# Streaming the expert weights past stationary tokens in the gate and up products of a mixture-of-experts layer

## The chip, the core and the metric

The kernel runs on one core of a Trainium2 chip. The metric is the device time of one launch in microseconds, the median of several runs. The engines of the core are named as in the profile: PE (TensorE, matrix products), PEld (its weight loads), DVE (VectorE), ACT (ScalarE), POOL (GpSimd) and SP (SyncE, which here only issues transfers). "Slot" means a 512 KB piece of on-chip memory that holds 128 rows of one expert's weights.

## The reference, cut to what matters

One layer of a diffusion backbone on 640 tokens of 1024 numbers, all float32. The part that the change touches is the grouped top-2 mixture of 16 experts at the end of the layer:

```python
def expert_block(args):
    xe, e = args
    return (jax.nn.silu(xe @ w_gate[e]) * (xe @ w_up[e])) @ w_down[e]
```

Every token goes to two experts. The rows are sorted by expert, padded to whole blocks, and each block is run through its expert's three 1024x1024 matrices. The rest of the layer (two token mixers, norms, router) comes before, and the weighted sum of each token's two rows and the last norm come after.

## The kernel before, in words

All engines run their own instruction list and meet at semaphores. The first 1100 us hold the mixers, the output projection and the router. Then the expert stage begins.

**Blocks.** The kernel cuts an expert's tokens into blocks of `MB` = 64. With this input there are 28 blocks; experts 0 to 15 have 1, 1, 1, 1, 2, 2, 2, 2, 4, 1, 3, 4, 1, 1, 1, 1 of them. Nine experts have one block, seven have two or more (19 blocks). The blocks run in the order of the experts.

**PE, lines 1566 to 1612.** For each block a loop over f (eight groups of 128 hidden columns) makes the gate and the up product for that f: the weights are the stationary operand, 128 rows by 64 columns at a time, and the 64 tokens stream (`mm` at L1603, 32 products for an f: 2 matrices, 8 row groups k, 2 halves of the array's columns). The result has hidden columns on partitions, so ACT applies silu (L711), DVE multiplies (L1222), and the product is at once the stationary operand of the down product `down(f)` (L1588), which runs one f behind: two products, each 64 tokens stationary and 512 weight columns streaming, one in either half of the array. At f = 7 the next block's tokens are transposed (`transpose_x`, L1571), and ACT copies them out (L702). Each float32 product is two records in the trace.

**Weights, lines 407 to 427.** An expert has 24 slots of 512 KB: for each f one of gate, one of up, one of down. There is one set of slots. SP issues the loads of the next expert in the order gate f, up f, down f: it waits until the last block of the expert before has used gate and up of f (`gu_done`), issues those two, waits for `down_done` of f, issues the third. SP issues strictly in its written order. PE waits at `gu_in[f]` and `dn_in[f]`. The first expert's loads wait for `h2_ready`, the last three of them for `x_scattered`.

**POOL, lines 470 to 545.** Early in the kernel it fills the sorted input rows and part of the output rows with zeros by transfers of 64 rows, and waits for them before it builds `m_lhs` (L487 to L494), which the scan of the first mixer (DVE, L905 to L913) doesn't need but runs beside. In the expert stage it loads the tokens of each block and stores the results `y_block`.

Of the kernel before, what the change touches and what calls it, by code (L numbers as in the profile page):

```python
# [26 lines left out]
ALU = mybir.AluOpType  # L27
ACT = mybir.ActivationFunctionType
AX = mybir.AxisListType

P = 128
# [57 lines left out]
def hybrid_step(nc, x_t, x_rows, pos_rows, small, const, masks, stream, w_out, norm_f, hg_state, router_w,  # L89
                w_gate, w_up, w_down, y_rows, s5_new, hg_new):  # L90
    ctx = ExitStack()
    with ctx:
# [116 lines left out]
        w_slot = [at(f"expert_w{s}", end - (s + 1) * 4096, [P, KD, P]) for s in range(3 * KF)]  # L209
        x_blk = at("x_block", qs0, [P, D])  # L210
        x_blk_t = at("x_block_t", qs0 + 4096, [P, KD, MB])
        act_t = at("act_t", qs0 + 8192, [P, KF, MB])
        y_blk = at("y_block", qs0 + 12288, [P, 512])
        silu = at("silu_tmp", qs0 + 16384, [P, 2, MB])
# [96 lines left out]
        silu_ready = sem("silu_ready")  # L311
        x3_ready = sem("x3_ready")
# [59 lines left out]
        def _(sp):  # L372
# [34 lines left out]
            sp.wait_ge(h2_ready, CH)  # L407
            for f in range(KF):
                if f == KF - 1:
                    sp.wait_ge(x_scattered, 16 * 2 * CH)  # L410
                sp.dma_start(w_slot[3 * f][:, :, :], w_gate[0, f, :, :, :]).then_inc(gu_in[f], 16)
                sp.dma_start(w_slot[3 * f + 1][:, :, :], w_up[0, f, :, :, :]).then_inc(gu_in[f], 16)
                sp.dma_start(w_slot[3 * f + 2][:, :, :], w_down[0, f, :, :, :]).then_inc(dn_in[f], 16)
            sp.wait_ge(route_ready, 1)
            with sp.Fori(1, EXPERTS) as e:
                b = sp.value_load(rint[0:1, bass.ds(e + START, 1)], min_val=0, max_val=NBLK)
                for f in range(KF):

                    sp.wait_ge(gu_done, b * KF + (f + 1))
                    sp.dma_start(w_slot[3 * f][:, :, :], w_gate[bass.ds(e, 1), f, :, :, :]  # L420
                                 .rearrange("a p k c -> p (a k) c")).then_inc(gu_in[f], 16)
                    sp.dma_start(w_slot[3 * f + 1][:, :, :], w_up[bass.ds(e, 1), f, :, :, :]
                                 .rearrange("a p k c -> p (a k) c")).then_inc(gu_in[f], 16)

                    sp.wait_ge(down_done, b * KF + (f + 1))
                    sp.dma_start(w_slot[3 * f + 2][:, :, :], w_down[bass.ds(e, 1), f, :, :, :]
                                 .rearrange("a p k c -> p (a k) c")).then_inc(dn_in[f], 16)
# [20 lines left out]
        def _(pool):  # L448
# [22 lines left out]
            for b in range(NBLK + 1):  # L471
# [1278 lines left out]
```

## Time and profile before

| | us |
|---|---|
| runs | 1858.84, 1854.5, 1855.0; median 1855.0 |
| profiled execution | 1854.49 |
| its span (first to last instruction) | 1852.9 |
| first gate product to end of the last down product | 1106.08 to 1804.77 |
| PE busy over the span | 1547.5 (84%) |
| gate and up products, busy / mean of one record | 460.7 / 0.224 |
| down products, busy / mean of one record | 229.7 / 0.602 |

The span is 1.6 us shorter than the execution's own time, which is 0.5 us below the median. Busy times of PE overlap: a product is counted from its start to the end of its result, so cadence is read from the starts in the timeline and not from the mean. The profile's chain of waits puts 63% of the span on PE, 19% on DVE and 9% on DMA.

### The profile page before, as it was taken

Reading aid. Unit: us, or ns where it says so; the run is one execution under the profiler, and the core shown is the slowest. Engines: PE = TensorE matmul, PEld = TensorE weight load, DVE = VectorE, ACT = ScalarE, POOL = GpSimd, SP = SyncE. Lnnn points to the kernel's source line nnn. Section 1 sums busy time; section 2 is a strip of 40 time slices with the busy share of each in tenths; the row PEclk is TensorE's granted clock in tenths of the full one; section 3 lists DMA queues with packets and bytes.
Section 4 is the critical chain, followed back from the end, with each engine's and each line's share of the span. In section 5 each row is a group of like instructions: output and inputs, shape, how many; then the busy total and the mean of one; then the engine's idle time right before and its main releaser. Section 6 shows DMA issues by size and latency. Waiting matters only on the chain.

```text
span 1852.9 us, 46239 instructions
## 1 busy us (share of the span) xinstructions
PE 1547.5 (84%) x20214; PEld 1206.8 (65%) x20215; DVE 581.4 (31%) x1109; ACT 265.2 (14%) x463; POOL 187.6 (10%) x212
## 2 busy tenths in 40 slices
PE   7598994997576787999989819889999998999770
PEld 7376793997466675777744617657777776777550
DVE  3812994002678855111153221001111110111006
ACT  2014000001322222000001101111111111111012
POOL 0043581001000000000000020000000000000002
PEclk9798996666789998999999759999999999999995
DMA  9059505123201110122301469988887194719984
GB/s 349 26 146 235 137 24 103 57 69 86 74 24 57 46 62 30 46 69 68 159 12 57 174 226 395 397 338 297 301 300 285 51 396 158 296 27 393 396 349 175
DMA packets 90295, 319.19 MB, mean 172 GB/s; under 512 B 11489, under 2 KB 14817, under 8 KB 89985
## 3 DMA queue, kind: packets, MB, share of 16 engines
q1 hardware_dynamic: 72288, 270.05, 38.8%
q0 software_dynamic: 14496, 46.77, 9.3%
q10 hardware_dynamic: 3456, 1.57, 0.8%
q8 instruction: 42, 0.69, 0.1%
q14 instruction: 13, 0.10, 0.0%
HBM read 283.46 MB, written 32.80 MB: 171 GB/s over the span
## 4 chain that ended last, share of the span: by engine, by line
PE 63%; DVE 19%; DMA 9%; SPq 4%; issue 3%; ACT 1%; ACTq 1%; POOL 1%; POOLq 0%; DVEq 0%
PE ps L1603 18%; PE ps L1277 13%; PE ps L1588 8%; DMA expert_w<-in_w_up 7%; PE ps L1295 4%; PE ps L1520 4%; PE ps L1540 4%; PE ps L1481 3%; DVE block_states L913 2%; DVE scan_tmp L905 2%; DVE scan_tmp L911 2%; PE ps L1418 2%; SPq L420 1%; DVE node_x L1044 1%; DVE node_x L1043 1%
## 5 line engine op out<-in xcount | busy, mean ns | idle before, releaser
L1603 PEld LDWEIGHTS ps<-x_block_t,expert_w 128*64 128x64 f32 x14336 | 453.5, 139 | 176.0 <-issue 105.0
L1603 PE MATMUL ps<-x_block_t,expert_w 128*64 128x64 f32 x14336 | 460.7, 224 | 49.2 <-DMA expert_w<-in_w_up 46.0
L1277 PE MATMUL ps<-h_t,weight_ring 128*128 128x320 f32 x1152 | 319.3, 438 | 21.0 <-DVE h_t L884 21.0
L1277 PEld LDWEIGHTS ps<-h_t,weight_ring 128*128 128x128 f32 x1152 | 222.2, 193 | 115.8 <-DVE h_t L884 21.5
L1222 DVE TENSOR_TENSOR act_t<-silu_tmp,ps 128x64 f32<-128x64 f32 x224 | 49.6, 222 | 596.6 <-ACT silu_tmp L711 596.6
L1588 PE MATMUL ps<-expert_w,act_t 128*64 128x512 f32 x896 | 229.7, 602 | 0.0
L711 ACT ACTIVATE silu_tmp<-ps 128x64 f32<-128x64 f32 x224 | 50.0, 223 | 583.0 <-PE ps L1603 583.0
L1295 PE MATMUL ps<-c_silu,weight_ring 128*128 128x128 f32 x768 | 123.8, 333 | 11.3 <-DMA weight_ring<-in_stream 11.3
L1295 PEld LDWEIGHTS ps<-c_silu,weight_ring 128*128 128x128 f32 x768 | 117.8, 244 | 12.1 <-issue 6.8
L1481 PE MATMUL ps<-node_x 128*128 128x128 f32 x560 | 73.3, 288 | 42.2 <-DVE node_x L1044 24.3
L1481 PEld LDWEIGHTS ps<-node_x 128*128 128x128 f32 x560 | 67.7, 199 | 47.8 <-DVE node_x L1044 27.0
L540 POOL DMA_DIRECT2D y_sorted<-y_block x56 | 29.9, 534 | 512.6 <-DVE y_block L1226 509.9
L1540 PE MATMUL ps<-w_out_sb,merged 128*128 128x512 f32 x160 | 68.8, 592 | 0.0
L524 POOL DMA_INDIRECT x_sorted<-h,router_ints x10 | 9.6, 962 | 558.5 <-DVEq L1215 555.8
L1588 PEld LDWEIGHTS ps<-expert_w,act_t 128*64 128x64 f32 x896 | 48.2, 139 | 17.9 <-issue 16.0
L1540 PEld LDWEIGHTS ps<-w_out_sb,merged 128*128 128x128 f32 x160 | 30.4, 190 | 38.3 <-issue 38.1
L648 ACT ACTIVATE exp_tmp<-exp_tmp 128x2560 f32<-128x2560 f32 x16 | 37.4, 2337 | 121.5 <-DVE exp_tmp L1035 59.9
L1571 PE MATMUL ps<-constants,x_block 64*128 64x64 f32 x232 | 20.9, 232 | 32.8 <-DMA x_block<-x_sorted 32.8
L941 DVE TENSOR_SCALAR k_fwd<-f_fwd 128x2560 f32<-128x2560 f32 x1 | 1.5, 1495 | 141.4 <-PE ps L1422 141.4
L913 DVE TENSOR_TENSOR block_states<-scan_tmp,scan_tmp 128x64 f32<-128x64 f32 (+1 forms) x63 | 42.3, 672 | 2.1
L1015 DVE COPY_PREDICATED att<-masks,ps 128x256 f32<-128x256 uint8 x70 | 35.1, 523 | 25.1 <-PE ps L1481 25.0
L1571 PEld LDWEIGHTS ps<-constants,x_block 64*128 64x128 f32 x232 | 16.9, 141 | 34.9 <-DMA x_block<-x_sorted 33.0
(301 smaller groups left out, 1451.9 us busy)
## 6 DMA issues: line engine op xcount, KB each, us to landing
expert_w<-in_w_gate SPq DMA_DIRECT2D x128, 512.0 KB, 13.5
expert_w<-in_w_up SPq DMA_DIRECT2D x128, 512.0 KB, 14.7
expert_w<-in_w_down SPq DMA_DIRECT2D x128, 512.0 KB, 14.2
weight_ring<-in_stream SPq DMA_DIRECT2D x98, 512.0 KB, 3.6
x_sorted<-zero POOLq DMA_DIRECT2D x36, 256.0 KB, 20.5
x_block<-x_sorted POOLq DMA_DIRECT2D x29, 256.0 KB, 6.6
y_sorted<-y_block POOLq DMA_DIRECT2D x56, 128.0 KB, 5.1
y_sorted<-zero POOLq DMA_DIRECT2D x19, 256.0 KB, 40.0
```

Of the source, the lines that this page charges most:

```text
L648: nc.scalar.activation(ex[:, :, :], ex[:, :, :], ACT.Exp).then_inc(e_exp, 1)
L711: nc.scalar.activation(silu[:, f % 2, :], ps[:, f % 2, 0:MB], ACT.Silu).then_inc(silu_ready, 1)
L913: done(vec.tensor_tensor(h_out, t1, t2, ALU.add))
L1222: vec.tensor_tensor(act_t[:, f, :], silu[:, f % 2, :], ps[:, 2 + f % 2, 0:MB], ALU.mult)\
L1277: last = mm(pair(job)[:, a, :], w[:, k, :], h_t[:, k, a * HALF:(a + 1) * HALF], start=(k == 0), stop=(k == KD - 1))
L1295: last = mm(bank(job)[:, 2 * j:2 * j + P], w[:, k, :], bc(csil[:, k, :], 1, P // 2), start=(k == 0), stop=(k == KD - 1))
L1481: last = mm(bank(job)[:, h * P:(h + 1) * P], both, both, start=True, stop=True)
L1520: last = mm(bank(job)[:, 0:HALF], br[:, 4 * w + k, :], y[:, k, a * HALF:(a + 1) * HALF], start=(k == 0), stop=(k == 3))
L1540: last = mm(bank(job), merged[:, k, c * P:(c + 1) * P], wo[:, k, 512 * half:512 * half + 512], start=(k == 0), stop=(k == KD - 1))
L1571: last = nc.tensor.transpose(ps[:, 6, k * MB:(k + 1) * MB], x_blk[0:MB, k * P:(k + 1) * P], ident[0:MB, 0:MB])
L1588: last = mm(ps[MB * half:MB * half + MB, 4, :], act_t[:, f, :], w_slot[3 * f + 2][:, 4 * half:4 * half + 4, :].rearrange("p k c -> p (k c) ...
L1603: last = mm(ps[cols, 2 * w + f % 2, 0:MB], w_slot[3 * f + w][:, k, cols], x_blk_t[:, k, :], start=(k == 0), stop=(k == KD - 1))
```

## The change

The expert stage is written in another way, and three things around it move.

- **Gate and up.** The tokens `x_block_t` are now the stationary operand, 64 columns, and 512 weight columns stream. For each of eight row groups k there are four products: two halves of the columns, and gate in the upper half of the array's columns, up in the lower. The result has tokens on partitions (gate in 0 to 63, up in 64 to 127), over two banks. ACT copies it to `gate_up_rows`, PE turns it with eight 128x128 transposes (`turn_rows`), ACT applies silu to all 512 columns at once, DVE multiplies all 512 at once.
- **Down.** The down product of block i-1 runs in iteration i, behind the gate and up products and the token transposes of block i. The first block's gate and up stand ahead of the loop, the last block's down behind it.
- **Weights.** A gate or up slot now holds 128 input rows of all 1024 columns. SP issues all 16 gate and up loads of an expert, each pair behind `gu_done` of the last block before, and then its 8 down loads, each behind `down_done`.
- **Around it.** The first expert's first 12 loads wait for `x2_ready` and no longer for `h2_ready`; the slots and the small tiles have other addresses. The zero fill goes by 128 rows (28 transfers, before 55). POOL stores the result of a block in the next iteration.

```diff
-            sp.wait_ge(h2_ready, CH)
+            sp.wait_ge(x2_ready, CH)
+            for k in range(KD):
+                if 2 * k == 12:
+                    sp.wait_ge(h2_ready, CH)
+                sp.dma_start(w_slot[2 * k][:, :], w_gate[0, k, :, :]).then_inc(gu_in[k], 16)
+                sp.dma_start(w_slot[2 * k + 1][:, :], w_up[0, k, :, :]).then_inc(gu_in[k], 16)
             for f in range(KF):
                 if f == KF - 1:
                     sp.wait_ge(x_scattered, 16 * 2 * CH)
-                sp.dma_start(w_slot[3 * f][:, :, :], w_gate[0, f, :, :, :]).then_inc(gu_in[f], 16)
-                sp.dma_start(w_slot[3 * f + 1][:, :, :], w_up[0, f, :, :, :]).then_inc(gu_in[f], 16)
-                sp.dma_start(w_slot[3 * f + 2][:, :, :], w_down[0, f, :, :, :]).then_inc(dn_in[f], 16)
+                sp.dma_start(w_slot[2 * KD + f][:, :], w_down[0, f, :, :]).then_inc(dn_in[f], 16)
...
             with sp.Fori(1, EXPERTS) as e:
-                b = sp.value_load(rint[0:1, bass.ds(e + START, 1)], min_val=0, max_val=NBLK)
+                last = sp.value_load(rint[0:1, bass.ds(e + START, 1)], min_val=0, max_val=NBLK)
+                for k in range(KD):
+
+                    sp.wait_ge(gu_done, last * KD + (k + 1))
+                    sp.dma_start(w_slot[2 * k][:, :], w_gate[bass.ds(e, 1), k, :, :]
+                                 .rearrange("a p c -> p (a c)")).then_inc(gu_in[k], 16)
+                    sp.dma_start(w_slot[2 * k + 1][:, :], w_up[bass.ds(e, 1), k, :, :]
+                                 .rearrange("a p c -> p (a c)")).then_inc(gu_in[k], 16)
                 for f in range(KF):
-                    sp.wait_ge(gu_done, b * KF + (f + 1))
...
-                    sp.wait_ge(down_done, b * KF + (f + 1))
...
+                    sp.wait_ge(down_done, last * KF + (f + 1))
+                    sp.dma_start(w_slot[2 * KD + f][:, :], w_down[bass.ds(e, 1), f, :, :]
+                                 .rearrange("a p c -> p (a c)")).then_inc(dn_in[f], 16)
...
-            for b in range(NBLK + 1):
-                pool.dma_start(x_sorted[b * MB:(b + 1) * MB, :], zero[0:MB, :]).then_inc(zeroed, 16)
+            for r in range(0, X_ROWS, P):
+                pool.dma_start(x_sorted[r:r + P, :], zero[:, :]).then_inc(zeroed, 16)
...
+            def rows():
+                nc.scalar.activation(gu_rows[:, :, :], ps[:, 0:2, :], ACT.Copy).then_inc(gu_taken, 1)
+
+            def gate():
+                nc.scalar.activation(silu[:, :, :].rearrange("p (a c) t -> p a c t", a=2),
+                                     ps[:, 2:4, :].rearrange("p a (c n) -> p a c n", c=4)[:, :, :, 0:MB], ACT.Silu)\
+                    .then_inc(silu_ready, 1)
...
+            with act.Fori(1, NBLK) as i:
                 with act.If(i < blocks):
...
+                    act.wait_ge(gu_done, i * KD + KD)
+                    rows()
                     act.wait_ge(xt_done, i + 2)
                     copy_x()
+                    act.wait_ge(prod_ready, i)
+                    act.wait_ge(gu_turned, i + 1)
+                    gate()
...
+            def turn_rows():
+                for f in range(KF):
+                    last = nc.tensor.transpose(ps[:, 2 + f // 4, f % 4 * P:f % 4 * P + P],
+                                               gu_rows[:, f // 4, f % 4 * P:f % 4 * P + P], ident)
+                last.then_inc(gu_turned, 1)
+
+            def gate_up(come, x_come):
+                for k in range(KD):
+                    pe.wait_ge(gu_in[k], come)
+                    if k == KD - 1:
+                        pe.wait_ge(x_blk_in, x_come)
+                    for h in range(2):
+                        for w in range(2):
+                            last = mm(ps[MB * w:MB * w + MB, h, :], x_blk_t[:, k, :],
+                                      w_slot[2 * k + w][:, 512 * h:512 * h + 512], start=(k == 0), stop=(k == KD - 1))
+                    last.then_inc(gu_done, 1)
+
+            def down(come):
+                for f in range(KF):
+                    pe.wait_ge(dn_in[f], come)
+                    for h in range(2):
+                        last = mm(ps[MB * h:MB * h + MB, 4, :], act_t[:, f, :],
+                                  w_slot[2 * KD + f][:, 512 * h:512 * h + 512], start=(f == 0), stop=(f == KF - 1))
+                    last.then_inc(down_done, 1)
...
+            pe.wait_ge(xt_copied, 1)
+            gate_up(32, 32)
+            transpose_x()
+            pe.wait_ge(gu_taken, 1)
+            turn_rows()
+            with pe.Fori(1, NBLK) as i:
                 with pe.If(i < blocks):
...
+                    gate_up(e * 32 + 32, i * 16 + 32)
+                    transpose_x()
+                    before = pe.value_load(rint[0:1, bass.ds(i - 1, 1)], min_val=0, max_val=EXPERTS - 1)
+                    pe.wait_ge(prod_ready, i)
+                    pe.wait_ge(y_copied, i)
+                    down(before * 16 + 16)
+                    pe.wait_ge(gu_taken, i + 1)
+                    turn_rows()
                 pe.nop()
+            pe.wait_ge(prod_ready, blocks)
+            pe.wait_ge(y_copied, blocks)
+            down(16 * EXPERTS)
```

**SP, the loads of the next expert.** In the loop over experts, SP's instructions before; `in_w_gate`, `in_w_up` and `in_w_down` are the three matrices in memory, and each row is one slot's load. The other six f read the same.

```order
L420 ISA [waits gu_done]
L420 DMA expert_w_126<-in_w_gate 128x1024
L422 DMA expert_w_127<-in_w_up 128x1024
L426 DMA expert_w_128<-in_w_down 128x1024 [waits down_done]
L419 REGISTER_ALU
L420 ISA [waits gu_done]
L420 DMA expert_w_129<-in_w_gate 128x1024
L422 DMA expert_w_130<-in_w_up 128x1024
L426 DMA expert_w_131<-in_w_down 128x1024 [waits down_done]
```

The same loop now, from the last gate and up pair to the loop's end and back.

```order
L428 ISA [waits gu_done]
L428 DMA expert_w_140<-in_w_gate 128x1024
L430 DMA expert_w_141<-in_w_up 128x1024
L435 DMA expert_w_142<-in_w_down 128x1024 [waits down_done]
L435 DMA expert_w_143<-in_w_down 128x1024 [waits down_done]
L435 DMA expert_w_144<-in_w_down 128x1024 [waits down_done]
L435 DMA expert_w_145<-in_w_down 128x1024 [waits down_done]
L435 DMA expert_w_146<-in_w_down 128x1024 [waits down_done]
L435 DMA expert_w_147<-in_w_down 128x1024 [waits down_done]
L435 DMA expert_w_148<-in_w_down 128x1024 [waits down_done]
L435 DMA expert_w_149<-in_w_down 128x1024 [waits down_done]
L423 REGISTER_ALU
```

What moved: the down loads stood among the gate and up loads, and now stand behind all of them; the next expert's first gate load stands behind the eighth down load.

**PE, a block's iteration.** Before, at the first two f of a block (L1603 gate and up, L1588 down).

```order
L1603 MATMUL ps<-x_block_t,expert_w_126 64x64 x16
L1603 MATMUL ps<-x_block_t,expert_w_127 64x64 x16
L1603 MATMUL ps<-x_block_t,expert_w_129 64x64 x16
L1603 MATMUL ps<-x_block_t,expert_w_130 64x64 x16
L1583 ISA
L1584 ISA
L1588 MATMUL ps<-expert_w_128,act_t 64x512 x2
L1603 MATMUL ps<-x_block_t,expert_w_132 64x64 x16
L1603 MATMUL ps<-x_block_t,expert_w_133 64x64 x16
```

Now, from the eighth row group of gate and up (L1635) to the second step of down (L1643, slots 142 and 143).

```order
L1632 ISA [waits gu_in7]
L1635 MATMUL ps<-expert_w_140,x_block_t 64x512 [waits x_blk_in]
L1635 MATMUL ps<-expert_w_141,x_block_t 64x512
L1635 MATMUL ps<-expert_w_140,x_block_t 64x512
L1635 MATMUL ps<-expert_w_141,x_block_t 64x512
L1618 MATMUL ps<-constants,x_block 128x64 x8
L1661 TENSOR_LOAD router_ints
L1641 ISA [waits y_copied,prod_ready]
L1643 MATMUL ps<-expert_w_142,act_t 64x512 [waits dn_in0]
L1643 MATMUL ps<-expert_w_142,act_t 64x512
L1643 MATMUL ps<-expert_w_143,act_t 64x512 [waits dn_in1]
```

What moved: 16 products of 64 columns for each slot became two of 512 columns, and the first down product of a block stands behind the whole gate and up of the next block.

## Rows read from the trace of the kernel before

**Rows 1.** The page's part 5: busy us, mean ns of one; idle before, releaser

```profile
L1603 PE MATMUL ps<-x_block_t,expert_w 128*64 128x64 f32 x14336 | 460.7, 224 | 49.2 <-DMA expert_w<-in_w_up 46.0
...
L1588 PE MATMUL ps<-expert_w,act_t 128*64 128x512 f32 x896 | 229.7, 602 | 0.0
```

**Rows 2.** Timeline of PE, a block without waits: start us, us, engine, line, op

```profile
1253.16 2.04 PE L1603 MATMUL ps<-x_block_t,expert_w 128*64 128x64 f32 x64
1255.02 1.03 PE L1588 MATMUL ps<-expert_w,act_t 128*64 128x512 f32 x4
1255.88 2.04 PE L1603 MATMUL ps<-x_block_t,expert_w 128*64 128x64 f32 x64
...
1268.75 0.71 PE L1571 MATMUL ps<-constants,x_block 64*128 64x64 f32 x8
1269.39 1.94 PE L1588 MATMUL ps<-expert_w,act_t 128*64 128x512 f32 x8
1271.15 1.04 PE L1603 MATMUL ps<-x_block_t,expert_w 128*64 128x64 f32 x30
```

**Rows 3.** Busy us by stretches (PE, PEld, DVE, ACT, POOL), then clock, DMA share, GB/s

```profile
1247.00:1269.50 22.50, 22.50 (x554) 17.76 (x552) 2.46 (x9) 3.58 (x11) 1.60 (x3) 1.00 0.82 288
1728.00:1760.00 32.00, 24.29 (x526) 17.95 (x523) 2.46 (x9) 3.67 (x10) 1.59 (x3) 0.95 1.03 400
```

**Rows 4.** Timeline of SP, the first loads of experts 14 and 15

```profile
1720.15 3.03 SPq L420 DMA_DIRECT2D expert_w<-in_w_gate  x1
...
1753.57 2.64 SPq L420 DMA_DIRECT2D expert_w<-in_w_gate  x1
```

**Rows 5.** Waits of SP's queue: us in total, times, longest

```profile
SPq L420 <- PE ps L1603: 276.0, 8, 67.6
SPq L426 <- PE ps L1588: 92.1, 71, 3.3
```

**Rows 6.** The slots' loads, from issue to landing

```profile
DMA to landing us min/median/max: 3.5/14.2/18.6
```

**Rows 7.** Timeline of PE, the start of the expert stage

```profile
1106.08 6.02 PE L1603 MATMUL ps<-x_block_t,expert_w 128*64 128x64 f32 x128 [0.77 <-ACT x_block_t L702]
```

**Rows 8.** 128x128 transposes at the full clock: ns min/median/max, first and last start

```profile
L1334 PE MATMUL ps<-constants,g_pre x64: 272/273/273, 146.1 to 153.0; 128*128 128x128 f32 x64
```

**Rows 9.** The chain of waits, eight 128x128 transposes at the half clock

```profile
1044.24 1.98 PE ps L1548 x8
```

**Rows 10.** ACT's copy of 128x1024 out of PSUM

```profile
L580 ACT ACTIVATE g_lhs<-ps x8: 1026/1054/1102, 147.2 to 153.5; 128x1024 f32<-128x1024 f32 x8
```

**Rows 11.** Timeline, the last block's down product and the copy of its result

```profile
1802.83 1.94 PE L1588 MATMUL ps<-expert_w,act_t 128*64 128x512 f32 x8
1802.93 0.60 ACT L702 ACTIVATE x_block_t<-ps 128x512 f32<-128x512 f32 x1 [0.41 <-PE ps L1571]
...
1804.90 0.69 DVE L1226 COPY y_block<-ps 128x512 f32<-128x512 f32 x1 [2.12 <-PE ps L1588]
```

**Rows 12.** Timeline of PE, two steps behind a wait for weights

```profile
1726.99 2.08 PE L1603 MATMUL ps<-x_block_t,expert_w 128*64 128x64 f32 x64 [2.36 <-DMA expert_w<-in_w_up]
...
1755.92 3.56 PE L1603 MATMUL ps<-x_block_t,expert_w 128*64 128x64 f32 x64 [2.33 <-DMA expert_w<-in_w_up]
```

**Rows 13.** Timeline of POOL, the zero fill and what waits for it

```profile
126.04 18.69 POOL L472 DMA_DIRECT2D x_sorted<-zero  x36 [0.29 <-POOL zero L470]
...
204.32 4.36 POOL L487 TENSOR_TENSOR m_lhs<-small_params,powers 128x2304 f32<-128x2304 f32 x1 [48.86 <-DMA y_sorted<-zero]
```

**Rows 14.** Timeline of DVE, the scan as POOL starts

```profile
204.30 0.22 DVE L911 TENSOR_TENSOR scan_tmp<-scan_tmp,block_states 128x64 f32<-128x64 f32 x1
204.55 4.21 DVE L913 TENSOR_TENSOR block_states<-scan_tmp,scan_tmp 128x64 f32<-128x64 f32 x1
```

**Rows 15.** Timeline of PE during the zero fill

```profile
162.47 5.93 PE L1347 MATMUL ps<-u_blocks,g_lhs 128*64 128x80 f32 x128 [3.43 <-issue]
172.52 1.06 PE L1347 MATMUL ps<-u_blocks,g_lhs 128*64 128x80 f32 x10 [4.11 <-issue]
```

More of the change, by code:

```diff
@@ L311, in hybrid_step @@
         silu_ready = sem("silu_ready")
+        gu_taken = sem("gu_taken")
+        gu_turned = sem("gu_turned")
         x3_ready = sem("x3_ready")
@@ L531, in _, with store_y @@
             blocks = pool.value_load(rint[0:1, TOTAL:TOTAL + 1], min_val=EXPERTS, max_val=NBLK)
-            with pool.Fori(0, NBLK) as i:
+            def store_y(row):
+                for half in range(2):
+                    pool.dma_start(y_sorted[bass.ds(row, MB), 512 * half:512 * half + 512],
+                                   y_blk[MB * half:MB * half + MB, :]).then_inc(y_stored, 16)
+            pool.wait_ge(xt_done, 1)
+            pool.dma_start(x_blk[0:MB, :], x_sorted[MB:2 * MB, :]).then_inc(x_blk_in, 16)
+            with pool.Fori(1, NBLK) as i:
                 with pool.If(i < blocks):
@@ L703, in copy_x @@
                     .then_inc(xt_copied, 1)
+            def rows():
[4 more added lines that the diff above has]
+                    .then_inc(silu_ready, 1)
             act.wait_ge(xt_done, 1)
             copy_x()
-            with act.Fori(0, NBLK) as i:
+            act.wait_ge(gu_done, KD)
+            rows()
+            act.wait_ge(xt_done, 2)
+            copy_x()
+            act.wait_ge(gu_turned, 1)
+            gate()
+            with act.Fori(1, NBLK) as i:
                 with act.If(i < blocks):
-                    for f in range(KF):
-                        act.wait_ge(gu_done, i * KF + f + 1)
-                        nc.scalar.activation(silu[:, f % 2, :], ps[:, f % 2, 0:MB], ACT.Silu).then_inc(silu_ready, 1)
+                    act.wait_ge(gu_done, i * KD + KD)
+                    rows()
                     act.wait_ge(xt_done, i + 2)
                     copy_x()
+                    act.wait_ge(prod_ready, i)
+                    act.wait_ge(gu_turned, i + 1)
+                    gate()
                 act.nop()
@@ L1217, in _, with product, take_y @@
             blocks = dve.value_load(rint[0:1, TOTAL:TOTAL + 1], min_val=EXPERTS, max_val=NBLK)
[L1218 to L1226 removed]
+            def product():
+                vec.tensor_tensor(act_t[:, :, :].rearrange("p (a c) t -> p a c t", a=2),
+                                  silu[:, :, :].rearrange("p (a c) t -> p a c t", a=2),
+                                  ps[:, 2:4, :].rearrange("p a (c n) -> p a c n", c=4)[:, :, :, MB:2 * MB], ALU.mult)\
+                    .then_inc(prod_ready, 1)
+            def take_y():
+                vec.tensor_copy(y_blk[:, :], ps[:, 4, :]).then_inc(y_copied, 1)
+            dve.wait_ge(silu_ready, 1)
+            product()
+            with dve.Fori(1, NBLK) as i:
+                with dve.If(i < blocks):
+                    dve.wait_ge(down_done, i * KF)
+                    dve.wait_ge(y_free, i)
+                    take_y()
+                    dve.wait_ge(silu_ready, i + 1)
+                    product()
                 dve.nop()
+            dve.wait_ge(down_done, blocks * KF)
+            dve.wait_ge(y_free, blocks)
+            take_y()
             w_of = rt[:, N_GS, 20:30]
```

83 lines of the change are left out of this document (22 added, 61 removed).

## The prediction

> **What bounds the kernel now.** I read four views, in this order. The page's part 5 first: the two largest groups of the stage are the gate and up products and the down products, and PE's idle time before the first is put down to the loads of up weights [rows 1]. Then the timeline of PE over one block that waits for nothing. The reader is to see the cadence in the starts: an f of gate and up takes 1.86 us (1253.16 to 1255.02), one of down 0.86 (1255.02 to 1255.88), the eight token transposes 0.64, and two steps of down 1.76 [rows 2]. A block is 8 x 1.86 + 8 x 0.86 + 0.64 + 0.2 for the loop = 22.6 us. 28 such blocks are 632.5 of the stage's 698.7 us (1106.08 to 1804.77). The other 66 are waits for weights, and the third view shows where. In the stretches, a block in the middle of many-block experts has PE busy throughout; in the stretch of single-block experts DMA is full at 400 GB/s and PE is busy 24.3 us of 32 [rows 3]. SP starts the loads of expert 14 at 1720.15 and of expert 15 at 1753.57 [rows 4]: 33.4 us for 24 loads, 1.39 us each. That is the floor of a single-block expert while the queue never runs empty. Fourth, SP's waits: eight long ones for gate and up, ahead of each expert whose loads wait through several blocks, and 71 short ones for down, 3.3 us at most [rows 5]. So the stage has two bounds: PE's 22.6 us a block where an expert has several, DMA's 33.4 us where it has one.
>
> **The change, part by part.** The sum runs from the first gate product to the end of the last down product.
>
> *Gate and up.* A k step is four products in the shape of today's down: 64 columns stationary, 512 streaming, in two halves of the array. Two such take 0.86 us [rows 2], so a step is 1.72 and all eight 13.76, against 14.9 now. The pairing in the two halves is seen in the 1.76 us for two steps of down in a row.
>
> *Turning the rows.* Eight more 128x128 transposes. The 64 in the trace at the full clock run from 146.1 to 153.0, 0.11 us each [rows 8], so 0.89 a block. Bounds: the token transposes' 0.64 [rows 2] and 1.98 at the half clock [rows 9]. I take 0.89, same shape and full clock.
>
> *A block that waits for nothing* is then 13.76 + 0.64 + 6.88 + 0.89 + 0.1 = 22.3 us, 0.3 less than now. ACT's copy of 1024 columns, 1.05 us [rows 10], lies under the 6.9 us of down. Silu and product of 512 columns, about 0.6 and 0.7 [rows 11], lie under the next 13.8 us of gate and up. If they were not covered they would cost up to 2.4 a block, but every wait of theirs has over 5 us of cover. The two register loads of PE's loop I cost in the 0.1; without cover, by today's 0.2 for the loop, 0.1 more.
>
> *The loads, and this is the large term.* SP now waits for `down_done` of the last block of expert e-1 before it may issue the down loads of e, and the gate and up loads of e+1 are queued behind that wait. The down of that last block runs one iteration late, behind the gate and up of the first block of e. If e has two blocks or more this costs nothing: the loads of e+1 aren't allowed before its last block anyway, they start with that block's first step, the last pair is there 3.5 + 15 x 1.39 = 24.4 us later, and PE wants it after 20.6 + 12.0. If e has one block, the slots of gate and up come free during its only gate and up product, but SP stands at the down wait. Nothing is issued until the down product, and the gate and up of e+1, which PE wants 7 us later, come behind eight down loads.
>
> Such a transition costs, from the end of the first down step to the same point one expert later: first landing 3.5 us after its issue on an idle queue [rows 6], 23 more at 1.39 = 32.0, then the last k step 1.72, the token transposes 0.64, the first down step 0.86, and 0.1 for semaphores: 38.8 us. Expert 0's down weights are loaded ahead, and expert 15 has no successor, so the experts that pay are 1, 2, 3, 9, 12, 13 and 14: seven times 38.8 = 271.6.
>
> *Head and tail.* The first iteration has no down: 13.76 + 0.64 + 0.5 (what is left of ACT's copy) + 0.89 = 15.8. The first two f today take 6.02 us instead of 3.73 on a cold PE [rows 7]; I keep these 2.3. The last down product now stands behind transposes, silu (0.60) and product (0.69) with nothing beside them [rows 11]: 6.88 + 1.5 = 8.4.
>
> *Sum.* 15.8 + 2.3 + 20 x 22.3 + 271.6 + 8.4 = 744.1 us, against 698.7: 45.4 longer.
>
> *Edits that I cost at nothing.* The first loads move ahead of `h2_ready`. The stage starts at the tokens' landing, well behind the weights, and the last three loads still end in time; bounds 0 and -2.4, the half-step stalls of today's first block. POOL's store one iteration later has 22 us of cover, and only the last one counts, which moves with the end. The zero fill has the same bytes in half as many transfers. Today it is issued from 126, and POOL waits 48.9 us for it, until 204.32 [rows 13]. If it lands sooner, `m_lhs` starts sooner, but no gain follows: POOL's operations hold DVE's scan wherever they lie (a scan step's 0.22 us becomes 4.21 as POOL starts [rows 14]), and the scan is longer than they are. What could gain is PE, which stands 3.43 and 4.11 us without a cause in the trace during the fill [rows 15]. Bounds 0 and -9; I take -1, nearer to the row with the same bytes.
>
> *A cold PE.* In a transition PE ends its down and turn about 7 us after the first down step and waits for its first gate and up pair until 3.5 + 9 x 1.39 = 16 us. So the clock will fall to 1.2 GHz. Today a step behind a 2.33 us wait took 3.56 us, and one behind 2.36 us took 2.08 [rows 12]. A cold k step is 3.44, longer than the 2.78 in which a pair arrives, so PE is then busy throughout and recovers as it did at the stage's start, within the first two f [rows 7], and it catches up before the eighth pair. Bounds: 0, and the rival below. I take 2 us in all. The Trainium skill ("TensorE: Matmul & The Clock Gate", section "Loop structure matters more than you think") says that a long wait for DMA between matmuls makes PE run them cold, which speaks against this change. By that rule alone the k steps of a transition would all be at 1.2 GHz, and the sum would be that of the cold rival.
>
> Together +45.4 - 1 + 2 = +46.4 on the profiled execution's 1854.5, which is 0.5 below the median of the runs: 1901 us, 2.5% slower.
>
> **The rivals.**
>
> *PE stays cold through the transitions.* k steps with 1.72 us of work in every 2.78 may keep the half clock. For it: the 3.56 us step. Against it: the stretch with 24.3 busy of 32 us had a clock of 0.95 [rows 3]. Then the last k step, the token transposes and the first down step take 1.7, 0.6 and 0.9 more, 3.2 in each of seven: +22, so 1923 us. Were the whole down product cold as well, the loads would starve by 2.7 more each, 1942.
>
> *The loads are not held.* The other side. If the gate and up loads of e+1 went out as their slots come free, the queue would never run dry. The two runs of single-block experts then each move four experts' weights: 133.6 us less the last down loads' 11.1 against 15.8 + 3 x 22.3 + 13.8 = 96.5 and 4 x 22.3 + 13.8 = 103 of PE: waits of 26 and 19.5. The sum would be 15.8 + 2.3 + 27 x 22.3 + 8.4 + 45.5 = 674, 25 less than now: 1830 us. It decides when SP reaches expert e+1's first gate load before the down product of the block before ends. For it: the slots are free. Against it: SP's order puts eight waits for down ahead of that load, and a queue's waits are served in order [rows 5]. Between the two, with about a third of the held time left, the change would come out even.
>
> *The four products of a step don't overlap as the down's two do.* The same 64 columns are loaded four times, and if each load stood between the products, the product would lose its cover. A step would be up to 8 x 0.14 us longer, 9 us a block in 21 blocks: 2090 us. Against it: two down steps in 1.76 us have the same loads at the same places [rows 2]. The Trainium skill ("TensorE: Matmul & The Clock Gate", section "The mechanism") has weight loads overlap running products only in another row group, and here all share one. By its figure for a load, 64 columns at 1.2 GHz or 0.053 us, an estimate is 8 x 8 x 0.053 = 3.4 us a block, about 1970. The trace doesn't agree for the down product.
>
> **How the numbers follow.** The forecast has 0.77, the cold PE 0.13, the loads that aren't held 0.05 and the case between 0.02, the products without overlap 0.03. The forecast's own bounds are -7 and +23 for the transposes in 21 blocks, -9 for the fill, some 6 to either side for landing times. I take 1886 to 1926 for 8 in 10, which holds the cold case up to its price. The change from 1855 that a measurement of this kernel can tell from none is about 0.3%, 5.6 us. Faster by more has 0.05, within 0.02, slower 0.93.
>
> **What would show it right or wrong.** In the profile of the changed kernel: a block between waits is 22.3 us long, the gate and up steps start 1.72 us apart, and a block's transposes of the rows take 0.9. Seven blocks are 38 to 40 us long, those of experts 2, 3, 4, 10, 13, 14 and 15, with PE idle 9 us before the first k step and then 1 us between steps. SP's longest waits for single-block experts are for down. DMA's share falls in these stretches from 1.03 to some 0.87. The prediction is wrong if these blocks take 33 us or less (the loads weren't held), if k steps behind the fifth are 3.4 us long (the cold PE), or if a block without waits is longer than 24 us. Ahead of 1106 us nothing should move by more than a few.

## The result, and the profile after

| | before | after |
|---|---|---|
| median of the runs, us | 1855.9 (4 runs, 1854.5 to 1858.84) | 1925.0 (4 runs, 1917.46 to 1928.17) |
| ratio, 95% interval | | 1.0364 (1.033 to 1.0398) |
| profiled execution, its span | 1854.49, 1852.9 | 1923.49, 1921.9 |
| expert stage: start, end, length | 1106.08, 1804.9, 698.8 | 1101.18, 1876.09, 774.9 |
| end of the stage to end of the span | 48.0 | 45.8 |

The change makes the kernel 3.6% slower: 69 us where 46 were forecast, 1.0 inside the upper edge of the range of 1886 to 1926. The end of the stage is read where DVE begins to copy the last result. In the profiled executions the 69.0 us are +76.1 in the stage, -4.9 ahead of it and -2.2 behind it. The forecast for the stage alone was +45.4 and 2 for a cold PE.

The page's part 5, groups of the expert stage (line, engine, operation; count | busy us, mean ns | idle before and what ended it), against [rows 1, 10]:

```profile
L1635 PE MATMUL ps<-expert_w,x_block_t 128*64 128x512 f32 x1792 | 421.4, 621 | 109.2 <-DMA expert_w<-in_w_up 97.2
L1643 PE MATMUL ps<-expert_w,act_t 128*64 128x512 f32 x896 | 198.6, 596 | 1.8 <-DVE act_t L1254 1.8
L725 ACT ACTIVATE gate_up_rows<-ps 128x1024 f32<-128x1024 f32 x28 | 28.6, 1023 | 512.2 <-PE ps L1635 512.2
```

PE's idle time for up weights went from 46.0 to 97.2 us. That is only part of the 76, so the next view has to tell the blocks apart. ACT copies each block's transposed tokens once; from copy to copy, in us, the 28 intervals are: 17.1, 17.2, **40.4, 40.5, 40.1**, 26.6, 22.7, 25.3, 22.6, 25.2, 22.6, 27.4, 23.0, four of 22.6, **40.0**, seven of 22.6, **40.0, 39.9, 40.0**. Behind the first two, which hold no down product, three kinds are there: seven of 40, five of 23.0 to 27.4, and the rest at 22.6 (one at 22.7).

The seven of 40 are the transitions behind single-block experts. The timeline of PE over the first (start us, us, engine, line, operation, and in brackets the idle time before):

```profile
1133.84 0.71 PE L1618 MATMUL ps<-constants,x_block 64*128 64x64 f32 x8
1134.48 7.09 PE L1643 MATMUL ps<-expert_w,act_t 128*64 128x512 f32 x32
1141.49 1.09 PE L1624 MATMUL ps<-constants,gate_up_rows 128*128 128x128 f32 x8
1152.99 8.55 PE L1635 MATMUL ps<-expert_w,x_block_t 128*64 128x512 f32 x24 [10.41 <-DMA expert_w<-in_w_up]
1162.15 1.94 PE L1635 MATMUL ps<-expert_w,x_block_t 128*64 128x512 f32 x8 [0.61 <-DMA expert_w<-in_w_up]
1164.71 1.94 PE L1635 MATMUL ps<-expert_w,x_block_t 128*64 128x512 f32 x8 [0.62 <-DMA expert_w<-in_w_up]
...
1172.40 1.94 PE L1635 MATMUL ps<-expert_w,x_block_t 128*64 128x512 f32 x8 [0.62 <-DMA expert_w<-in_w_up]
1174.27 0.71 PE L1618 MATMUL ps<-constants,x_block 64*128 64x64 f32 x8
```

PE stands 10.4 us before the first k step, runs three steps in a row without a wait, and stands 0.6 before each one from the fourth on: there it takes pairs as they land, one every 2.57 us. The timeline of SP over the same stretch shows why they land late:

```profile
1135.60 6.34 SPq L435 DMA_DIRECT2D expert_w<-in_w_down  x8
1143.17 0.34 SPq L428 DMA_DIRECT2D expert_w<-in_w_gate  x1
1143.61 0.38 SPq L430 DMA_DIRECT2D expert_w<-in_w_up  x1
```

The eight down loads go out one by one as the late down product frees their slots, and the first gate load comes only behind them, though its slot had been free since the first step of the gate and up product that began at 1119.3. SP's waits (us in total, times, longest) say the same, against [rows 5], in which the down waits were 92.1 us in total and 3.3 at most:

```profile
SPq L435 <- PE ps L1643: 365.6, 120, 23.8
SPq L428 <- PE ps L1635: 182.1, 64, 46.7
```

The stretches of this transition and one without waits (busy us of PE, PEld, DVE, ACT, POOL; then granted clock, DMA share, GB/s), against [rows 3]:

```profile
1134.50:1142.00 7.50, 7.50 (x38) 2.69 (x38) 0.39 (x1) 0.96 (x2) 0.00 (x0) 1.00 0.66 206
1142.00:1153.00 11.00, 0.59 (x7) 0.36 (x5) 0.99 (x2) 0.60 (x1) 1.61 (x3) 0.65 1.02 414
1153.00:1174.30 21.30, 18.19 (x65) 4.63 (x65) 0.00 (x0) 0.00 (x0) 0.00 (x0) 0.86 0.86 329
1500.00:1522.00 22.00, 22.00 (x112) 7.98 (x110) 1.38 (x2) 2.11 (x3) 1.59 (x3) 1.00 0.73 258
```

The transfers are at half rate while PE works down, full while PE stands: the two no longer overlap. The clock falls to its half level while PE stands (granted 0.50 from 1146 to 1159 us, 0.65 as a mean of the stretch) and is back at 1.00 from 1159 on. The first three k steps take 8.55 us where three take 5.2 at the full clock.

The five intervals of 23 to 27 are something else. The chain of waits through the first of them, and the same place in the second:

```profile
1255.55 7.04 PE ps L1643 x32
1262.61 0.70 DVE y_block L1260
...
1264.56 5.82 DMA y_sorted<-y_block
...
1271.61 6.49 DMA x_block<-x_sorted
1278.09 0.04 issue
1278.14 3.40 PE ps L1635 x8
...
1320.77 6.84 DMA x_block<-x_sorted
1327.61 0.04 issue
1327.66 1.94 PE ps L1635 x8
```

Down product, copy, store of the result, its landing, then POOL's next load, which is the tokens of the next block: they arrive when PE already stands at its last k step. No weight is in this part of the chain.

A block that waits for nothing (timeline of PE), against [rows 2]:

```profile
1503.13 1.09 PE L1624 MATMUL ps<-constants,gate_up_rows 128*128 128x128 f32 x8
1504.16 13.95 PE L1635 MATMUL ps<-expert_w,x_block_t 128*64 128x512 f32 x64
1518.04 0.71 PE L1618 MATMUL ps<-constants,x_block 64*128 64x64 f32 x8
1518.68 5.80 PE L1643 MATMUL ps<-expert_w,act_t 128*64 128x512 f32 x26
```

From start to start: gate and up 13.88, token transposes 0.64, and on to the next turn, down and turn 8.1. A k step is 13.88 / 8 = 1.74.

Ahead of the stage, the timelines of POOL and PE against [rows 13, 15]:

```profile
126.55 9.47 POOL L481 DMA_DIRECT2D x_sorted<-zero  x18 [0.30 <-POOL zero L479]
136.01 5.24 POOL L484 DMA_DIRECT2D y_sorted<-zero  x10
172.81 4.30 POOL L497 TENSOR_TENSOR m_lhs<-small_params,powers 128x2304 f32<-128x2304 f32 x1 [31.57 <-DMA y_sorted<-zero]
...
160.97 4.65 PE L1394 MATMUL ps<-u_blocks,g_lhs 128*64 128x80 f32 x128 [1.48 <-issue]
167.45 0.63 PE L1394 MATMUL ps<-u_blocks,g_lhs 128*64 128x80 f32 x10 [1.83 <-issue]
```

The fill lands at 172.8, 31.5 us sooner, and two of PE's pauses shrink from 3.43 and 4.11 to 1.48 and 1.83.

### The profile page after: what moved, and what is told of

The parts are those of the page before. It is cut to its first block, busy times and chain, and to the rows that moved or that the text cites. A ratio compares the mean times of both kernels' runs of the same rounds, so it can differ in the third digit from the quotient of the medians.

```text
span 1921.9 us, 20334 instructions
## 1 busy us (share of the span) xinstructions
PE 1560.5 (81%) x7894; PEld 932.7 (49%) x7895; DVE 550.3 (29%) x913; ACT 221.6 (12%) x267; POOL 171.8 (9%) x185
## 4 chain that ended last, share of the span: by engine, by line
PE 59%; DVE 18%; DMA 11%; SPq 4%; issue 3%; ACT 1%; ACTq 1%; POOL 1%; POOLq 0%; DVEq 0%
PE ps L1635 13%; PE ps L1324 13%; PE ps L1643 10%; DMA expert_w<-in_w_up 7%; PE ps L1342 4%; PE ps L1567 4%; PE ps L1587 4%; PE ps L1528 3%; DVE block_states L948 2%; SPq L428 2%; DVE scan_tmp L940 2%; SPq L430 2%; DMA x_block<-x_sorted 2%; DMA y_sorted<-y_block 2%; PE ps L1465 2%
## 5 line engine op out<-in xcount | busy, mean ns | idle before, releaser
L1635 PE MATMUL ps<-expert_w,x_block_t 128*64 128x512 f32 x1792 | 421.4, 621 | 109.2 <-DMA expert_w<-in_w_up 97.2
L1635 PEld LDWEIGHTS ps<-expert_w,x_block_t 128*64 128x64 f32 x1792 | 125.8, 142 | 383.9 <-issue 233.1
L1260 DVE COPY y_block<-ps 128x512 f32<-128x512 f32 x28 | 19.4, 692 | 692.3 <-PE ps L1643 692.3
L1643 PE MATMUL ps<-expert_w,act_t 128*64 128x512 f32 x896 | 198.6, 596 | 1.8 <-DVE act_t L1254 1.8
L1643 PEld LDWEIGHTS ps<-expert_w,act_t 128*64 128x64 f32 x896 | 62.3, 137 | 115.5 <-issue 111.6
L725 ACT ACTIVATE gate_up_rows<-ps 128x1024 f32<-128x1024 f32 x28 | 28.6, 1023 | 512.2 <-PE ps L1635 512.2
L1050 DVE COPY_PREDICATED att<-masks,ps 128x256 f32<-128x256 uint8 x70 | 35.1, 523 | 25.2 <-PE ps L1528 25.1
L940 DVE TENSOR_TENSOR scan_tmp<-block_states,decay_re 128x64 f32<-128x64 f32 (+1 forms) x63 | 36.9, 586 | 17.6 <-ACT block_states L630 15.5
```

Of the source, the lines that this page charges most:

```text
L940: note(vec.tensor_tensor(t1, h_in, bc(arep[:, :], 1, m), ALU.mult))
L1635: last = mm(ps[MB * w:MB * w + MB, h, :], x_blk_t[:, k, :], w_slot[2 * k + w][:, 512 * h:512 * h + 512], start=(k == 0), stop=(k == KD - 1))
L1643: last = mm(ps[MB * h:MB * h + MB, 4, :], act_t[:, f, :], w_slot[2 * KD + f][:, 512 * h:512 * h + 512], start=(f == 0), stop=(f == KF - 1))
```

## Experiments

Three sets, each on one chip beside its own runs of the kernel before, whose medians were 1856.04 (13 runs), 1853.15 (17) and 1853.35 (11). All times are medians of runs, stages and intervals come from one profiled execution of each. The two kernels without loads ran once each, and that execution is the profiled one. Code is cut to what matters; in the first diff the register loads are put in words.

| kernel | median, us | ratio to before, 95% | stage, us |
|---|---|---|---|
| set 1: `sp_order` | 1840.5 (10) | 0.9922 (0.9899 to 0.9946) | 697.0 |
| set 1: `x_first` | 1903.3 (4) | 1.0238 (1.0181 to 1.0294) | 760.7 |
| set 1: `both` | 1815.7 (4) | 0.9796 (0.9748 to 0.9845) | 678.3 |
| set 1: `after_fill64` | 1924.6 (4) | 1.0362 (1.0319 to 1.0404) | 780.3 |
| set 2: `before_order` | 1908.8 (4) | 1.0302 (1.0262 to 1.0342) | 755.9 |
| set 2: `before_fill128` | 1841.7 (12) | 0.9947 (0.9924 to 0.997) | 699.4 |
| set 2: `before_noload` | 1786.5 (1) | | 635.2 |
| set 2: `after_noload` | 1786.0 (1) | | 636.5 |
| set 3: `after_rep` | 1917.3 (6) | 1.0341 (1.031 to 1.0373) | 777.8 |
| set 3: `fill64_rep` | 1928.4 (6) | 1.0408 (1.038 to 1.0437) | 781.3 |

**The order of SP's loads (`sp_order`).** The changed kernel, but where expert e has one block, the gate and up loads of e+1 are issued ahead of the down loads of e.

```diff
+            pairs(1, START of expert 1)
+            with sp.Fori(1, EXPERTS - 1) as e:
+                last, then = START[e], START[e + 1]
+                with sp.If(then < last + 2):
+                    pairs(e + 1, then)
+                    downs(e, last)
+                with sp.If(last + 1 < then):
+                    downs(e, last)
+                    pairs(e + 1, then)
+            downs(EXPERTS - 1, START of the last)
```

> Theory A (held loads): a single-block expert's transition is 40 us long because the next expert's gate and up loads stand behind eight waits for the down product in SP's order. Here SP puts the gate and up loads of e+1 ahead of the down loads of e where e has one block, and keeps the order elsewhere. The queue then runs through two series of four experts, 4 x 33.4 less the last down loads' 11.1 = 122.5 us each, against 98.9 and 104.3 us of PE: waits of 24 and 18 us in place of 7 x 17.4 = 122. The time falls by about 80 us to 1845 (1835 to 1860); no block is longer than 34 us. Theory B (the transition is as long as 24 loads on a busy queue and a cold PE make it, whatever the order): 1915 or more, the transitions stay above 38 us.

Measured 1840.5, and the stage is 697.0, 78 shorter. The intervals behind single-block experts are now 25.2, 29.3, 32.7, 24.8, 24.9, 25.1 and 31.8 instead of seven of 40. Not one product of PE was changed, so the held loads are shown to be what makes the transitions long. What is left are waits for tokens and, shorter, for weights (PE's waits, us in total, times, longest), and DMA's own floor of 32 to 33 us for a single-block expert (33.4 in [rows 4]).

```profile
PE ps L1651 <- DMA x_block<-x_sorted: 24.2, 13, 3.1
PE ps L1651 <- DMA expert_w<-in_w_up: 17.9, 20, 2.1
```

**POOL's order (`x_first`).** The changed kernel, but POOL issues the load of the next block's tokens ahead of its wait for the stored result (the first iteration stands ahead of the loop; in this form it holds for fewer than 35 blocks).

```diff
+            with pool.Fori(1, NBLK - 1) as j:
+                with pool.If(j + 1 < blocks):
+                    pool.wait_ge(xt_done, j + 2)
+                    pool.dma_start(x_blk[0:MB, :], x_sorted[bass.ds(j * MB + 2 * MB, MB), :]).then_inc(x_blk_in, 16)
+                with pool.If(j < blocks):
+                    pool.wait_ge(y_stored, j * 32)
+                    pool.sem_inc(y_free, 1)
+                with pool.If(j + 1 < blocks):
+                    pool.wait_ge(y_copied, j + 2)
+                    store_y(j * MB)
```

> Theory C (late tokens): in the changed kernel POOL loads a block's tokens only when the result of an earlier block is stored, 6 us behind the down product, and where weights are loading too the tokens land after PE wants them; five blocks are 0.4 to 4.8 us longer than 22.6, 14.6 in all. Here POOL issues the token load ahead of that wait. The time falls by 12 to 16 us to about 1911, and the two-block experts' blocks are 22.6 us. Rival D (these blocks wait for weights, which share the queue, and the tokens only land last): within 4 us of 1925.

The stage is 760.7, 14.2 shorter, and behind the first two every interval that isn't a transition is 22.6; the seven transitions stay at 40.0 to 41.0. Both halves of the theory hold: the five long blocks were late tokens, and these have no part in the transitions. The median is 22 lower, where 12 to 16 were expected. Between the two profiled executions, 19.0 us apart, 14.2 lie in the stage and 6.1 ahead of it (it starts at 1095.07 instead of 1101.18), where this kernel has the same instructions. So the stage confirms the expectation, and the rest is put down to the spread of executions ahead of it (below).

**Both edits (`both`).**

> The two edits together. Theory A and C: their gains add up, since one is in the transitions and the other in the blocks between: 1925 - 80 - 15 = 1830 (1818 to 1845), 1 to 2% faster than the kernel before. Theory B and D: 1910 or more. A third: with the queue full throughout, the tokens land later than now, and the gain of the second edit is lost: 1845.

1815.7: 2.0% faster than the kernel before, and 2 us below the low end of what was expected. The stage is 678.3, 20.5 shorter than before. Not all of the 2.0% is the schedule's: this kernel has the new zero fill too, which by itself takes 11 us off the kernel before (`before_fill128`, 1841.7). Against that kernel `sp_order` with 1840.5 is about even, and `both` some 26 us faster, read across chips. Behind the first two, its intervals are 22.6 but for 32.7, 32.7, 24.2, 27.1 and 32.6, where single-block experts stand in a row. The stretch of one of them, in which DMA is full:

```profile
1134.00:1166.00 32.00, 25.69 (x118) 7.34 (x114) 1.38 (x2) 2.11 (x3) 1.59 (x3) 1.00 1.03 401
```

**The load order in the kernel before (`before_order`).** PE's work as before, but SP issues all sixteen gate and up loads of an expert and then its eight down loads.

```diff
                     sp.dma_start(w_slot[3 * f + 1][:, :, :], w_up[...]).then_inc(gu_in[f], 16)
-
+                for f in range(KF):
                     sp.wait_ge(down_done, b * KF + (f + 1))
```

> The kernel before, with SP issuing all gate and up loads of an expert and then its down loads, as the changed kernel does; PE's order is untouched, so the down product of an expert's last block ends with that block. Theory A (the cost is the down product one block late together with SP's order): the down waits are over when SP comes to them, no load is held for long, and only the down weights of a single-block expert land later than now, behind its 16 other loads: its block grows from 33 to 35 to 38 us, the time by 5 to 25 us, to 1860 to 1880. Rival G (SP's order alone does it): transitions of 40 us and 1910 or more.

Measured 1908.8: a miss in size, by 29 over the upper end, and in place. It is near the 1910 of rival G, but not by G's mechanism: no interval is 40, the longest is 37.2. Most of the wait is PE's for down weights, 88.8 us in 15 waits. The first block of each expert waits for its *down* weights behind its first two f, which the old product order wants early. Timeline of PE over the starts of two such blocks:

```profile
1154.05 3.90 PE L1603 MATMUL ps<-x_block_t,expert_w 128*64 128x64 f32 x128
1169.86 1.97 PE L1588 MATMUL ps<-expert_w,act_t 128*64 128x512 f32 x4 [11.91 <-DMA expert_w<-in_w_down]
...
1191.25 3.90 PE L1603 MATMUL ps<-x_block_t,expert_w 128*64 128x64 f32 x128
1201.17 1.98 PE L1588 MATMUL ps<-expert_w,act_t 128*64 128x512 f32 x4 [6.01 <-DMA expert_w<-in_w_down]
```

So this run doesn't isolate the held loads, as it was meant to. What it shows is that the order in which loads are issued has to be the order in which PE takes them: gate and up ahead of down is right only for a schedule in which down comes late, as in the changed kernel.

**No weight loads.** In both kernels the loads of experts 1 to 15 are left out; all blocks use expert 0's weights. The diff is that of the kernel before.

```diff
-            with sp.Fori(1, EXPERTS) as e:
-                ...
-                        pe.wait_ge(gu_in[f], e * 32 + 32)
+                        pe.wait_ge(gu_in[f], 32)
```

> The kernel before without the weight loads of experts 1 to 15; all blocks use expert 0's weights. PE alone: 28 blocks of 22.6 us, the stage 636 us long (699 now).

> The changed kernel without the weight loads of experts 1 to 15. Theory A: without loads nothing is held, each block is 22.6 us, the stage 17.2 + 27 x 22.6 + 9 = 636 us, the same as the kernel before without loads; the products' new shape by itself neither gains nor costs. By the prediction's term of 22.3 a block it would be 628. Theory C adds that the tokens are in time, since stores and token loads have the queue to themselves: no block over 22.7 us. If they are late here too, the lateness is POOL's order alone, and about 2.5 us show in every block.

Stages of 635.2 and 636.5 us. Without weights to wait for, the new shape of the products gains nothing and loses nothing: behind the first two all intervals are 22.6 in both. The late tokens are gone as well, though POOL's order is the changed one: they are late only while their transfers share the DMA engines with the weights (a load of tokens lands in 3.4 us at the median without weights, in 6.5 with them). All but 1 of the 76 us between the stages are thus made of waits. The weights cost 698.8 - 635.2 = 63.6 us before, and 774.9 - 636.5 = 138.4 after; in `both` they cost 41.8.

**The zero fill.** `before_fill128` is the kernel before with the fill by 128 rows; `after_fill64` and `fill64_rep` are the changed kernel with the old fill by 64; `after_rep` is the changed kernel once more.

```diff
-            for b in range(NBLK + 1):
-                pool.dma_start(x_sorted[b * MB:(b + 1) * MB, :], zero[0:MB, :]).then_inc(zeroed, 16)
+            for r in range(0, X_ROWS, P):
+                pool.dma_start(x_sorted[r:r + P, :], zero[:, :]).then_inc(zeroed, 16)
```

> The kernel before with the zero fill of 128 rows a transfer. Theory E: the fill lands near 173 us in place of 204, PE's pauses beside it fall from 9.0 to about 5 us, and the time falls by 4 to 10 us. Rival F: within 3 us of before, the difference at 350 us being lost again in PE's clock behind it.

> The changed kernel with the zero fill of before (55 transfers of 64 rows in place of 28 of 128). Theory E: the expert stage starts 4.9 us sooner in the changed kernel because the faster fill shortens PE's pauses without a cause at 153 to 173 us; with the old fill they are 9.0 us again, the stage starts at 1106, and the time is 4 to 6 us longer, about 1930. Rival F: the earlier start comes from the earlier weight loads at the end of the output projection: the pauses come back, but the stage still starts near 1101 and the time stays at 1925.

> The changed kernel itself once more, beside the next run on the same chip, since the fill's effect was only compared across chips so far. 1915 to 1927.

> The changed kernel with the old zero fill, on the same chip as the changed kernel itself. Theory E: the fill of 128 rows brings in the changed kernel what it brought in the kernel before (11 us there), so this run is 6 to 13 us slower than the changed kernel. Rival F: in the changed kernel it brings nothing, as the first run of this edit reads (1924.6 against 1925.0 on another chip): within 3 us.

In the kernel before, the new fill wins 11.5 us (1841.7 against 1853.15), a little more than the 4 to 10 expected. In the changed kernel, on one chip, the old fill costs 11.1 (1928.4 against 1917.3). The first try, `after_fill64`, had been inconclusive: 1924.6 stood against the 1925.0 of another chip, and a difference of 11 us (0.6%) can't be read across sets. Its trace spoke for theory E all the same: the pauses are back (5.87 and 4.05) and the stage starts at 1108.30, not near 1101. Timelines of POOL, PE and DVE in `before_fill128`:

```profile
174.48 4.45 POOL L488 TENSOR_TENSOR m_lhs<-small_params,powers 128x2304 f32<-128x2304 f32 x1 [33.14 <-DMA y_sorted<-zero]
...
164.58 0.63 PE L1348 MATMUL ps<-u_blocks,g_lhs 128*64 128x80 f32 x10 [0.51 <-issue]
...
283.55 0.22 DVE L912 TENSOR_TENSOR scan_tmp<-scan_tmp,block_states 128x64 f32<-128x64 f32 x1
```

PE's last group of these products starts at 164.58 instead of 172.52 [rows 15], and the scan, whose start waits for ACT's copies of PE's results (12.4 us instead of 21.4), begins at 166.60 instead of 174.96 and has its last step on L912 at 283.55 instead of 292.59. The scan itself takes 117.0 us instead of 117.6 although POOL's operations begin 30 us sooner beside it, so 9.0 of the 11.5 us are there, 8.4 of them the earlier start.

## Why the prediction was right, and where it was off

| part of the stage | forecast, us | measured, us |
|---|---|---|
| first gate product to the next block's | 15.8 + 2.3 | 1119.30 - 1101.18 = 18.1 |
| 20 blocks at 22.3, with no waits | 446.0 | 20 x 22.57 = 451.4 |
| seven transitions | 271.6 | 280.8 |
| tokens that come late | 0 | 14.6 |
| last turn, silu, product, down | 8.4 | 8.9 |
| sum (not accounted for: 1.1) | 744.1 | 774.9 |

The range held by 1.0 us, less than the spread of the runs (1917.46 to 1928.17), so that the time fell inside it is in part luck. The mechanism and its large term were right; the stage was 30.8 us longer than the sum, and nearly half of that is a term that the sum put at nothing.

**The held loads: right in place, kind and count, 3% small.** All seven transitions came where the sum put them, at 40.1 instead of 38.8. Of the 1.3 each, 1.2 are in the loads: the last of 24 landed 36.7 us after the first was issued (1135.60 to 1172.28) instead of 35.5. The excess is in the first ten, of which the tenth was there after 17.3 instead of 16.0; the rest came at 1.38 each. Whether the pace of the down product, at which the first eight are issued, or the result and the tokens, which go in the same stretch, make the 1.3 isn't settled. `sp_order` shows the mechanism by taking it away.

**The block: 22.3 forecast, 22.57 measured.** The step is 1.74 instead of 1.72, the turn 1.02 instead of 0.89, down 7.03 instead of 6.88. These are small errors of one sign over 20 blocks, 5.4 us. The gain of 0.3 us a block over the kernel before didn't come, and the runs without loads show it: 635.2 against 636.5.

**The step that failed: "POOL's store one iteration later has 22 us of cover, and only the last one counts".** The store had its cover; what stood behind it had not. POOL's loop waits for the stored result before it issues the next load of tokens. In both kernels PE asks for the tokens ahead of the last step of gate and up. Before, only a block's last two down steps came behind the token transposes and ahead of the copy of the result; the load was out at 1280.0 and the last step began at 1289.4, so 9.3 us for a landing of 6.6. Now all eight down steps lie between the transposes and the copy, 5.3 us more:

```profile
1280.04 0.53 POOL L536 DMA_DIRECT2D x_block<-x_sorted  x1 [6.11 <-issue]
...
1289.37 2.03 PE L1603 MATMUL ps<-x_block_t,expert_w 128*64 128x64 f32 x64
```

These two are timelines of the kernel before; the same two places after:

```profile
1271.61 0.53 POOL L554 DMA_DIRECT2D x_block<-x_sorted  x1 [6.51 <-issue]
...
1278.14 3.40 PE L1635 MATMUL ps<-expert_w,x_block_t 128*64 128x512 f32 x8 [2.38 <-DMA x_block<-x_sorted]
```

The load is out at 1271.6 and wanted at 1275.8, so 4.2 us for 6.5, and the step behind the wait is slow besides (3.40 instead of 1.94, at a granted clock of 0.50 from 1280.0 to 1281.5). Over five blocks that is 14.6 us; `x_first` took 14.2 away by moving the load ahead of the wait. The prediction had named POOL's queue as one that the moved step passes, and costed the instruction instead of what is queued behind its wait.

**The fill: 1 us forecast, 11 measured, 2 beyond the bound of 9 that was set aside.** "The scan is longer than they are" was true of POOL's operations and beside the point: the scan is fed by PE, and PE's pauses during the fill are what shrank. The pauses had been put at -9 as a bound, and the choice went to the wrong end. In the profiled pair only 4.9 us of it showed: there the stretch of 350 to 460 us took back some (below). On medians of one chip the changed kernel is 64 us slower (1917.3 against 1853.35), which is a stage 76 to 79 longer (774.9, and 777.8 in `after_rep`), less 11 for the fill and 2 behind the stage. The total was nearer to the forecast than the stage because these errors had opposite signs.

**The rivals.** *PE stays cold*: wrong. Behind the wait three steps were slow, and from the fourth on each took its 1.94 to the end of its result, as in a stretch without waits, though PE stood 0.6 us before each. By the clause of the prediction, 3.4 us behind the fifth step would have shown it. The slow steps cost nothing visible, as forecast, since pairs came no faster than they were used, and the 2 us set aside for them weren't needed. The Trainium skill ("TensorE: Matmul & The Clock Gate", section "Loop structure matters more than you think") has a long wait for DMA leave PE cold. The trace agrees for the wait of 10.4 us (granted 0.50), and with the waits of 0.6 between steps the clock was at 1.00 from 1162 to 1174. *The loads are not held*: it wasn't so in this kernel. Its price was sound: 674 for the stage, and `both`, which is this rival made real, has 678.3; `sp_order`, with late tokens, has 697.0. *The four products don't overlap*: wrong, a step is 1.74, so the loads of its stationary columns are as hidden as the down product's.

## What to carry to other kernels

Where a step is moved later, every queue that waits for it holds everything written behind that wait: list for each queue, the one that stores results too, what the next instruction feeds, and put loads whose slots are already free ahead of the wait. Loads have to be issued in the order in which the consumer takes them, so an order of the products and an order of the loads are changed together: here the same schedule was 3.6% slower with one order and, with two queues reordered and no product touched, 2.0% faster, 0.6 of it by the zero fill. When the stage is bound by waits, a shape of product that is a little cheaper is worth nothing until they are gone.

## What the runs showed of the hardware

- **Zeros by 128 rows instead of 64.** One issue by POOL takes 0.52 to 0.53 us in either (9.47 for 18, 18.69 for 36), so half as many cost half the time, and the same bytes, 14.4 MB, are landed 46.3 us after the first issue (126.55 to 172.81) instead of 78.3: 311 GB/s against 184. The Trainium skill ("SBUF — State Buffer", section "Door 1: The DMA port swizzle") states that partitions 0 to 63 reach only 8 of the 16 ports that DMA has into SBUF, and gives 196 GB/s for a transfer of 1 MiB on them against 328 for all 128 partitions. The trace is 5 to 6% below both rates. An estimate from these two figures of the Trainium skill is 73.6 us against 44.0 for the fill, some 30 sooner; the prediction sized the term without it.
- **PE pauses without a cause in the trace while the fill runs**: 1.47, 3.43 and 4.11 us with transfers of 64 rows (the last two in [rows 15]), 1.46, 5.33 and 3.89 in `fill64_rep`, 1.47, 1.48 and 1.83 in the changed kernel, 1.47 and 0.51 in `before_fill128`. What PE stands for there was not found out.
- **The clock in 350 to 460 us differs between executions.** In six executions with the same instructions up to the expert stage its mean was granted at 0.64 to 0.75 there, and the start of the stage goes with it: 1101.18 (changed kernel) and 1102.65 (`after_noload`) at 0.64, 1091.31 to 1095.07 (`sp_order`, `after_rep`, `x_first`) at 0.66 to 0.67, 1083.49 (`both`) at 0.75. That is a spread of 19 us, and why the clock differs is open. One profiled execution can't show an effect of 11 us ahead of the stage; medians of six runs on one chip did.
- **Transfers of 512 KB** were landed every 1.28 us (a pair each 2.57) while nothing else ran, 1.36 to 1.39 with tokens and results beside them.
